# Two RMS norms whose low parts are all made by VectorE, two tiles behind their products

## The reference

```python
def rms_norm(x, g):
    xf = x.astype(jnp.float32)
    y = xf * lax.rsqrt(jnp.mean(xf * xf, axis=-1, keepdims=True) + EPS)
    return (y * g.astype(jnp.float32)).astype(x.dtype)

def hybrid_layer(x, norm_mix_g, w_in, ...):
    h = rms_norm(x, norm_mix_g)                                   # norm "n1"
    aq, ak, av, hq, hf, hi, hg, ga, gh = split_combined(h @ w_in)
    ...
    x = x + merged @ w_out
    x = x + peer_layer(rms_norm(x, norm_ffn_g), w_peer_q, ...)    # norm "n2"
```

## Time and profile before

| | us |
|---|---|
| three runs: median (lowest to highest) | 2398.07 (2394.65 to 2405.0) |
| the profiled execution, its own time | 2392.5 |
| its span | 2390.7 |
| VectorE, first product to end of last low part, n1 | 22.20 to 34.28 |
| the same, n2 | 511.39 to 523.46 |
| first product of TensorE in the stage behind n1, behind n2 | 34.75, 524.08 |

### The profile page before, as it was taken

The page is one execution under the profiler, slowest core; times in us unless marked ns, Lnnn a source line. Parts: engine busy times, 40 slices in busy tenths (PEclk is TensorE's granted clock), DMA queues, the critical chain, the costliest instruction groups (busy, mean ns, idle before and its releaser), DMA issues. The chain is left out here.

```text
span 2390.7 us, 24408 instructions
## 1 busy us (share of the span) xinstructions
PE 2052.6 (86%) x8044; PEld 1366.0 (57%) x8044; DVE 1566.4 (66%) x3438; ACT 482.8 (20%) x1080; POOL 836.5 (35%) x637
## 2 busy tenths in 40 slices
PE   5998689969798989998988888898776579989977
PEld 4875468748547966555555555555322257724445
DVE  4568746449999956666666666666777775347652
ACT  3344122122112310000000000000000221335541
POOL 3420034333110026665555445455665232300002
PEclk8988589989899989999999999999988789999999
DMA  7976879668473679999999999999999322100001
GB/s 280 352 282 201 309 290 384 234 251 272 159 286 114 224 295 400 403 403 403 402 402 402 402 403 404 402 402 402 402 402 400 133 94 63 53 22 1 1 36 70
DMA packets 203900, 648.09 MB, mean 271 GB/s; under 512 B 19840, under 2 KB 52736, under 8 KB 202496
## 3 DMA queue, kind: packets, MB, share of 16 engines
q1 hardware_dynamic: 118384, 335.60, 37.7%
q0 software_dynamic: 73728, 268.47, 28.5%
q10 hardware_dynamic: 11664, 42.47, 5.2%
HBM read 560.48 MB, written 85.98 MB: 270 GB/s over the span
## 5 line engine op out<-in xcount | busy, mean ns | idle before, releaser
L1591 PE MATMUL ps<-arena 128*128 128x512 f32 x1024 | 516.1, 651 | 143.7 <-DVE arena L1448 99.3
L1459 DVE CUSTOM_DVE_ANT_0 arena<-arena 128x1024 bf16<-128x1024 f32 x256 | 313.6, 1226 | 247.9 <-DMA arena<-u_rows,u_row 134.4
L1580 PE MATMUL ps<-rows_n,arena 128*128 128x256 f32 x2048 | 464.7, 379 | 0.0
L1580 PEld LDWEIGHTS ps<-rows_n,arena 128*128 128x128 f32 x2048 | 386.9, 190 | 95.9 <-issue 50.0
L1591 PEld LDWEIGHTS ps<-arena 128*128 128x128 f32 x1024 | 206.7, 208 | 397.9 <-issue 261.7
L1323 POOL DMA_INDIRECT arena<-u_rows,u_row x256 | 286.6, 1119 | 313.4 <-DMA gates<-arena 168.3
L1323 POOL DMA_INDIRECT arena<-in_v,expert x192 | 209.7, 1092 | 320.6 <-DVE arena L1480 294.0
L1480 DVE SCALAR_TENSOR_TENSOR arena<-arena,wt 128x1024 f32<-128x1024 f32 x192 | 246.2, 1282 | 0.5
L1557 ACT ACTIVATE ge<-dots 128x2 f32<-128x2 f32 x128 | 26.0, 203 | 909.8 <-DVE dots L1459 909.8
L190 DVE STREAM_TRANSPOSE tdst<-tsrc 128x1024 f32<-128x1024 f32 x128 | 154.7, 1228 | 77.7 <-DMA tsrc<-in_u 41.1
L234 POOL TENSOR_TENSOR in_wlo<-in_raw,in_whi 128x1024 fp32r<-128x1024 f32 x45 | 115.2, 2562 | 228.1 <-ACT in_whi L230 228.1
(11 more groups left out here) (390 smaller groups left out, 2946.0 us busy)
## 6 DMA issues: line engine op xcount, KB each, us to landing
tsrc<-in_u SPq DMA_DIRECT2D x128, 512.0 KB, 7.7
u_rows<-tdst SPq DMA_DIRECT2D x128, 512.0 KB, 6.3
arena<-in_u SPq DMA_DIRECT2D x128, 512.0 KB, 10.6
arena<-in_v SPq DMA_DIRECT2D x128, 512.0 KB, 11.7
in_raw<-in_panels ACTq DMA_DIRECT2D x37, 512.0 KB, 3.8
gates<-arena SPq DMA_DIRECT2D x8, 2048.0 KB, 8.8
arena<-gates SPq DMA_DIRECT2D x32, 512.0 KB, 18.8
mg_raw<-in_panels ACTq DMA_DIRECT2D x28, 512.0 KB, 6.7
```

What stands on the lines that cost most here:

```text
L1459: nc.vector.tensor_tensor_reduce(out=junk[:, n % 2], in0=u_slot[n % NU], in1=hrows[:, n // NPICK], scale=1.0, scalar=0.0, op0=ALU.mult, op ...
L1580: mm = nc.tensor.matmul(ps[:, j % 2, 0:TD], ud[:, j % RJ, k], rows_n2[:, 0, k], start=k == 0, stop=k == KD - 1)
L1591: mm = nc.tensor.matmul(ps[:, 4 + 2 * t + c], park[:, j % NPK, t * P:(t + 1) * P], vd[:, j % RJ, c * T:(c + 1) * T], start=j == 0, stop=j ...
```

## The change

The two norms that make low parts have all eight of them made by VectorE. The low part of tile k - 2 stands ahead of the product of tile k for every k from 2 on, and those of tiles 6 and 7 stand at the end. GpSimd keeps only the low parts of the two weight panels. The ring's wait ahead of product k (k from 4, first norm only) is now always for VectorE's own low part of tile k - 4. The separate semaphore of GpSimd's low parts is gone.

```diff
@@ norm_stage, VectorE
                 for k in range(kt):
-                    if dst is None and k >= 3 and k % 2:
+                    if dst is None and k >= 2:
                         v.wait_ge(hi_ready, k - 1)
                         make_lo(k - 2)
                     if dst is None and keep is None and k >= 4:
-                        v.wait_ge((lo_pool, lo_dve)[k % 2], (k - 4) // 2 + 1)
+                        v.wait_ge(lo_dve, k - 3)
...
                 if dst is None:
-                    v.wait_ge(hi_ready, kt)
-                    make_lo(kt - 1)
-
-            if dst is None:
+                    for k in range(kt - 2, kt):
+                        v.wait_ge(hi_ready, k + 1)
+                        make_lo(k)
+
+            if ahead is not None:
                 @block.gpsimd
                 def _(pool):
-                    if ahead is not None:
-                        for i in range(2):
-                            ahead.make_lo(pool, i)
-                    for k in range(0, kt, 2):
-                        pool.wait_ge(hi_ready, k + 1)
-                        nc.gpsimd.tensor_tensor(both(dst_lo[:, k]), normed(k), both(dst_hi[:, k]).bitcast(F32),
-                                                ALU.subtract).then_inc(lo_pool, 1)
+                    for i in range(2):
+                        ahead.make_lo(pool, i)
```

More of the change, by code:

```diff
@@ L261, in both @@
                 return x if keep is None else x.rearrange("p (a t) -> p a t", a=2)
-            sq_act, sq_dve, sum_step, seeded, y_ready, hi_ready, lo_pool, lo_dve, dve, stored = sems(
-                st, " ".join(name + s for s in ("_sq_act", "_sq_dve", "_sum_step", "_seeded", "_y", "_hi", "_lo_pool", "_lo_dve", "_dve", "_stored")))
+            sq_act, sq_dve, sum_step, seeded, y_ready, hi_ready, lo_dve, dve, stored = sems(
+                st, " ".join(name + s for s in ("_sq_act", "_sq_dve", "_sum_step", "_seeded", "_y", "_hi", "_lo_dve", "_dve", "_stored")))
             block = st.enter_context(nc.Block())
```

## The result

The changed kernel takes 2404.17 us (median of 20 runs, 2397.87 to 2410.63), the kernel before in the same comparison 2394.65 us (20 runs, 2392.04 to 2409.34). The ratio is 1.003, 95% interval 1.002 to 1.0041: slower by 0.3%, where 0.12% faster was forecast. The profiled execution has a span of 2396.1 us, 5.4 us more than before. So these two traces account for 5.4 us of a difference of 9.5 between the medians.

What follows compares the result with a forecast made beforehand. It took the program as stages with different limits, VectorE alone setting the path in both edited norms. A gain of 1.49 us per norm, 3.0 us for both, gave 2398.07 - 3.0 = 2395.1 us, range 2388.5 to 2402.

Steps and rivals of the forecast that it cites:

- The norms: Both edited norms: VectorE's stretch from first product to last low part shrinks from 12.08 us, gaining 1.49 us each.
- The pair that no row of before had shown: In the edited norms, one low part then one product on VectorE: 1.28 us, with bounds up to 1.50 us.
- chained starts: Rival, edited norms: VectorE instructions carrying waits don't overlap, gain only 0.1 us per norm, 2397.9 us; chance 0.06.
- the stretching: VectorE instructions in the edited norms lengthened beside GpSimd's subtractions; 3.24 us per norm, expected to go with them.
- the rival that put it on the low part: Edited norms: each of eight low parts takes 1.64 us for 0.69, 12.2 us late for both, 2410.3 us; chance 0.02.
- What carries to the end: Stages behind the two norms: they start earlier by the gain, and 3.0 us reach the program's end.
- its end moves with its start: Said of the projections behind the first norm, filled to 98.7% by TensorE: the first norm's gain passes through.
- what the earlier trace could swallow: Rival: stages behind waiting for expert-row transfers swallow one norm's gain (2396.6 us) or both (2398.1 us); chance 0.15.
- the passing of work between engines: Claimed limit of the first attention stage, with no engine full: DVE 109.40 and PE 107.38 of 140.00 us.
- I can't derive from any row: Catch-all: a shift in the stages behind worth more than the norms themselves, either way; chance 0.05.

Runs made afterwards that it cites:

- pad_back: Changed kernel plus two unused VectorE instructions of 0.72 us each at the end of each of the two norms; 1.0016 against the kernel before.
- before_late: Kernel before plus 0.72 us of unused VectorE work at the end of the second block's norm; 1.0028 against the kernel before, 2406.54 us.
- n1_later: Kernel before plus 1.9 us of unused VectorE work at the end of the first norm; 1.0021 against the kernel before, 2399.71 us.
- three_late: Changed kernel plus the same edit at the second block's norm and 1.2 us of unused VectorE work behind it; 0.9978 against the kernel before, 2397.50 us.
- after_late: Changed kernel plus 2.7 us of unused VectorE work at the end of the second block's norm; 1.0002 against the kernel before, 2400.93 us.

## Why the prediction was wrong
**The norms.** Right. Forecast 1.49 us per norm; measured 12.08 - 10.51 = 1.57 in each. Forecast 10.6 to 10.8 us from first product to last low part, measured 10.51, just under it. The pair that no row of before had shown takes 1.27 us for the 1.28 taken from its lower bound; chained starts (1.50) are out. With GpSimd gone, every stretched instruction is at its clean length, so the stretching belonged to GpSimd and the rival that put it on the low part is out. TensorE's product at the second norm came at 520.16, forecast 521.1; of its 3.9 us, 3.1 are the norms' and 0.8 an earlier start of the first product (21.37 for 22.20), which no edit explains.

**What carries to the end.** This is the step that failed: "its end moves with its start". For the stage of which it was said it nearly held (TensorE starts it 2.4 us earlier, and the first maximum behind it comes 1.9 us earlier); it fails where I let it stand for all the stages behind. In the first pair of traces it held to the norm of the second block (4.2 us ahead at 1908.6), and what the earlier trace rows could swallow was not swallowed. The other traces don't bear that out. The four of kernels with both norms changed reach that norm at 1908.6, 1915.4, 1919.7 and 1920.8 us (mean 1916.1), the four with nothing edited up to there at 1912.8, 1915.7, 1916.3 and 1916.4 (mean 1915.3): as far as four traces each can say, nothing of the 3 us is left there, and the first attention stage, 2.8 us longer in the mean where the first norm is shortened, can account for that. Behind both norms I took every stage's length as fixed. It isn't: the same instructions, shifted, take 7.3 us more in the second attention stage, because the granted clock falls to half there for 17 us, and 2.2 us more in the stages ahead of it. The profile of before had the warning, and I passed over it: in the earlier trace rows the first attention stage stands at a clock of 0.67 and the stretches of the two norms at 0.57 and 0.53, so the clock does move between its levels in this kernel, and TensorE bounds or co-bounds the stages where it does. I had put the first attention stage down to the passing of work between engines; at a granted clock of 0.50 TensorE is busy there for 10.00 of 10.00 us. In the rival list this was only the 0.05 "I can't derive from any row"; with a price (a stage of TensorE at half speed for 10 to 20 us) it should have been the slower rival in place of the stretched low part, and the range should have reached 7 to 9 us above the kernel before.

**The range.** It was placed on a median of three runs, 2398.07 us; twenty runs in the same comparison put the kernel before at 2394.65, and the three later groups at 2398.47, 2398.15 and 2393.99. The result, 2404.17 us, lies 2.2 us above the range. The scatter within one kernel, 10 to 20 us, I took for noise of measurement. Much of it goes with the clock: each run has a mean granted clock on record, and within every kernel the longer runs have the lower one (correlation -0.46 in pad_back, -0.68 to -0.94 in all others). The twenty runs of the changed kernel make the same picture: six at 2397.9 to 2399.2 us with 0.919 to 0.921, fourteen at 2401.9 to 2410.6 with, but for three, 0.917 or less. In which stage each lost it no record shows, since one execution of a kernel has a trace.

**What is shown and what stays open.** Shown: in the traces the loss lies at half clock in stages that the edit doesn't touch; the edit isn't needed for it (before_late, n1_later); it can be removed with the edit in place (three_late, and by its trace after_late). Not shown: why the changed kernel arrives at the second block so that it falls more often, and why the place of the return decides over a fall 200 us behind it. pad_back has the old timing up to 645 us and still arrives on the losing side, and how often each kernel does so would take many more traces. Also not tried: giving TensorE work in its idle time ahead of either attention stage, to see whether its clock then stays up.

## What to carry to other kernels
An edit that saves 3 us in a program of 2400 can be outvoted by the clock of a stage far behind it. Before a loss is put down to an edit, compare the length of every stage and the granted clock in it; where a length differs with the same instructions, shift the start by a fraction of a microsecond of empty work in both kernels and time them again. Take more than one trace of each: two executions of the same changed kernel differed by 12 us here (spans of 2396.1 and 2408.2). And where the profile page shows the granted clock below 1 in a stage that TensorE helps to bound, give "this stage runs at the other level" a chance and a price.

## What the runs showed of the hardware
- 0.72 us of VectorE work that nothing uses made the kernel 0.28% (0.1 to 0.47%) slower, 6.7 us by the ratio. 2.7 us of it in another kernel cost nothing that twelve runs could find (mean 3.1 us less, give or take 4.1).
- In the changed kernel the fall came 1.6 us into the attention stage (2138.84 for a first product at 2137.24), after 34.1 us at full clock in which TensorE was busy for 33.2, its longest pause the 0.94 us ahead of the stage. Ahead of those, around the start of the stage before, it had stood at half clock, idle for part of the time: 10.2 us in all five traces that fell behind it, 6.8 us in all eight that didn't.
- In each of the two norms three of GpSimd's four subtractions of 128x512 cost a VectorE instruction with its operands in on-chip memory 0.95 to 1.0 us and the fourth 0.29 us (1.1 us in the norm of the second block); where the subtractions were gone, nothing was lost. This agrees in kind with the rule of the Trainium skill ("SBUF — State Buffer", section "Who interferes with whom").
